# Where the on-chip buffers of a two-block transformer kernel begin: all large buffers moved to multiples of 2048 bytes, the arena to a multiple of 512

## The chip, the core and the metric

The kernel runs on one core of one Trainium2 chip. The metric is the device time of one execution in microseconds (us), as the median of several. A core has five engines that run side by side and wait for each other with semaphores: TensorE (PE in the profile; its weight loads are shown apart as PEld), VectorE (DVE), ScalarE (ACT), GpSimd (POOL) and SyncE (SP, which here only issues DMAs). On-chip memory (SBUF) has 128 partitions; a buffer takes the same byte range in each, so "begins at 16512" means byte 16512 of every partition. TensorE reads both operands of a matmul from SBUF, the stationary one with LDWEIGHTS and the moving one with MATMUL, and writes its sums to a bank of PSUM (2 KB in each partition).

## The reference, cut to what matters

Two transformer blocks at SEQ = 256 rows of D = 1024, all in float32:

```python
h = rms_norm(x, g_mix);  proj = h @ w_in                      # 1024 -> 8192
ya = rms_norm(diff_attention(qa, ka, va)) ;  yr = silu(gr) * rms_norm(retention(qr, kr, vr))
x = x + (sigmoid(gate_a) * (ya @ w_branch_diff) + sigmoid(gate_r) * (yr @ w_branch_ret)) @ w_out
x = x + square(relu(rms_norm(x) @ w_ff1)) @ w_ff2              # 1024 -> 4096 -> 1024
x = x + sigmoid(rms_norm(x) @ w_ple_gate) * (p @ w_ple)
x = rms_norm(x)                                                # end of block 1
x = x + 0.5 * (silu(n(x) @ w_gate) * (n(x) @ w_up)) @ w_down   # 1024 -> 2816 -> 1024
x = x + concat(mla(...), moba(...)) @ w_out2
x = x + 0.5 * (silu(n(x) @ w_gate2) * (n(x) @ w_up2)) @ w_down2
out = rms_norm(x)
```

## The kernel before, in words

**Precision.** A float32 matrix product is made from three matmuls of a rounded type (fp32r): each operand is split into a high and a low part, and high x high, high x low and low x high are summed in PSUM.

**Weights.** All weights go through one list of 164 units of up to 128 x 2048 float32 (1 MB each). SP loads unit u into `raw[u % 6]` (`load`, L324), two DMAs each; ScalarE copies it rounded into `w_hi[u % 4]` (`hi`, L909, instruction L917); VectorE writes the difference into `w_lo`, which lies on top of `raw` (`lo`, L1300, instruction L1306). The weights are the moving operands of the matmuls.

**Activations.** They are the stationary operands, 128 x 128 at a time. TensorE turns a 128 x 128 block by a transpose against the identity in `masks` (`turn`, L472, instruction L478) into a PSUM bank; ScalarE writes the rounded part (`split`, L923) and VectorE the rest (L1313). Each turned operand has a home of its own: `hA` and `hB` hold the 1024-wide operands of the projections, `fT` the inner activations of the three feed-forward layers on their way down, `pT` the operand of w_ple, `cT` those of the two up-projections of the latent attention (384 columns of weights at a time for the queries, 512 for keys and values).

**Products.** All weight products go through `products` (L455), whose matmul is L464. A "narrow" product has 512 (or 384, 288) weight columns and one PSUM bank per 128 rows; a "wide" one has 1024 columns of weights, and so two matmuls of 512 columns, into two banks, for each stationary operand. Every matmul has its own LDWEIGHTS. The order on each engine is written out by hand; TensorE waits for `lo_ready` of a unit, ScalarE and the SP queue wait for `unit_used`.

**Where buffers lie.** `sb` (L170) hands out addresses one after the other, each rounded up to 32 bytes, from `nc.sbuf_base` (16481) rounded up to 128, which is 16512. The order is `raw`, `w_hi`, `hA`, `hB`, `x`, `src`, `gain`, `junk`, then two small scratch buffers, `masks`, some twenty small vectors, and last the arena (L208), a region that the stages of the kernel use in turn through `lay` (L210). The start of the arena is whatever was left:

```python
    at = [-(-nc.sbuf_base // 128) * 128]                       # 16512
    raw = [sb(f"raw{s}", [P, UNIT]) for s in range(RAW_SLOTS)]
    arena = at[0]                                              # 160160
    fT0, fT1, act_r, act_f, pl_s, sg, pT0, pT1, p_sb, gain_mid = lay(arena, ("fT_hi", [P, 4, SEQ], f32r), ...)
    (cT0,), (cT1,) = (lay(named[where], ...) for where, name in (("qT", "cT_hi"), ("kT", "cT_lo")))
```

Summed up from these lines, with the remainders that matter:

| buffer | begins, before | modulo 2048 | modulo 64 | begins, after | modulo 2048 |
|---|---|---|---|---|---|
| raw0 (w_lo0) | 16512 | 128 | 0 | 18432 | 0 |
| w_hi0 | 65664 | 128 | 0 | 67584 | 0 |
| hA_hi / hB_hi | 98432 / 114816 | 128 | 0 | 100352 / 116736 | 0 |
| x, src, gain | 131200, 139392, 147584 | 128 | 0 | 133120, 141312, 149504 | 0 |
| masks | 154496 | 896 | 0 | 155648 | 0 |
| arena, fT_hi, qaT | 160160 | 416 | 32 | 160256 | 512 |
| act_f | 172448 | 416 | 32 | 172544 | 512 |
| pT_hi | 192928 | 416 | 32 | 193024 | 512 |
| cT_hi | 202400 | 1696 | 32 | 202496 | 1792 |

All blocks that a matmul takes from `hA`, `hB`, `fT`, `pT` and `cT` lie at multiples of 512 bytes from the start of their buffer, so each keeps the remainder modulo 64 of its buffer.

Of the kernel before, what the change touches and what calls it, by code (L numbers as in the profile page):

```python
# [28 lines left out]
P = 128  # L29
D, TB, SEQ = 1024, 2, 256  # L30
KT = D // P
EPS = 1e-6
BIG = 1e30
RAW_SLOTS, HI_SLOTS = 6, 4
UNIT = 2048
HALF = 512


DH, DHD = 8, 64
RH, RK, RV = 4, 128, 256  # L40
# [52 lines left out]
def work_batches():  # L93
# [16 lines left out]
    order += [("p",)]  # L110
    order += [("ff", i, tb) for i in range(DFF // HALF) for tb in range(TB)]
    order += [("ple", tb, h) for tb in range(TB) for h in range(2)]
# [46 lines left out]
def two_blocks(nc, x_d, p_d, g_mix, w_in, lam_q1, lam_k1, lam_q2, lam_k2, g_diff, g_ret, w_bd, w_br, w_out,  # L159
# [3 lines left out]
    f32, f32r, bf16, i32 = mybir.dt.float32, mybir.dt.float32r, mybir.dt.bfloat16, mybir.dt.int32  # L163
# [3 lines left out]
    at = [-(-nc.sbuf_base // 128) * 128]  # L167
    named = {}

    def sb(name, shape, dt=f32, where=None):  # L170

        size = (2 if dt == bf16 else 4) * int(np.prod(shape[1:]))
        if where is None:
            where = at[0]
            at[0] += -(-size // 32) * 32
        named[name] = where
        return nc.alloc_sbuf_tensor_at(name, shape, dt, offset=where)

    raw = [sb(f"raw{s}", [P, UNIT]) for s in range(RAW_SLOTS)]
    w_lo = [sb(f"w_lo{s}", [P, UNIT], f32r, named[f"raw{s}"]) for s in range(RAW_SLOTS)]  # L180
    w_hi = [sb(f"w_hi{s}", [P, UNIT], f32r) for s in range(HI_SLOTS)]

    hA = [sb(f"hA_{s}", [P, KT, SEQ], f32r) for s in ("hi", "lo")]
    hB = [sb(f"hB_{s}", [P, KT, SEQ], f32r) for s in ("hi", "lo")]
    x = sb("x", [P, TB, D])
    src = sb("src", [P, TB, D])
    gain = sb("gain", [P, D])
    junk = sb("junk", [P, D], bf16)
    vjunk = sb("vjunk", [P, P], bf16)
    rjunk = sb("rjunk", [P, RV], bf16)  # L190
    masks = sb("masks", [P, P + 2 * 384])
    ident, mask, negdist = masks[:, 0:P], masks[:, P:P + 384], masks[:, P + 384:P + 768]
    ss = sb("ss", [P, 2 * len(NORMS)])
    rs = sb("rs", [P, 2 * len(NORMS)])
    ms = sb("ms", [P, 2 * len(NORMS)])
# [6 lines left out]
    ssc, msc, rsc = (sb(n, [P, 4]) for n in ("ssc", "msc", "rsc"))  # L202
    mn = sb("mn", [P, 32, TB])
    sm = sb("sm", [P, 32, TB])
    rsm = sb("rsm", [P, 32, TB])
    qc = sb("qc", [P, DH, TB])
    gd = sb("gd", [P, P])
    arena = at[0]  # L208

    def lay(start, *parts):  # L210

        out = []
        for name, shape, *dt in parts:
            out.append(sb(name, shape, dt[0] if dt else f32, start))
            start += -(-4 * int(np.prod(shape[1:])) // 32) * 32
        assert start <= nc.sbuf_usable_end, (name, start)
        return out
# [6 lines left out]
    (gg,) = lay(arena, ("gg", [P, TB, D]))  # L224
    qk_tm = lay(named["yr"], ("qk_tm0", [P, TB, HALF]), ("qk_tm1", [P, TB, HALF]))
    lam_v, lam_w = lay(named["ga"], ("lam_v", [P, 4, DHD]), ("lam_w", [P, 2, DHD]))
# [6 lines left out]
    fT0, fT1, act_r, act_f, pl_s, sg, pT0, pT1, p_sb, gain_mid = lay(  # L233
        arena, ("fT_hi", [P, 4, SEQ], f32r), ("fT_lo", [P, 4, SEQ], f32r), ("act_r", [P, TB, HALF]),
        ("act_f", [P, TB, HALF]), ("pl_s", [P, TB, D]), ("sg", [P, TB, D]),
        ("pT_hi", [P, 2, SEQ], f32r), ("pT_lo", [P, 2, SEQ], f32r), ("p_sb", [P, TB, 256]), ("gain_mid", [P, D]))
# [19 lines left out]
    ctx = ExitStack()  # L256
    bank = [ctx.enter_context(nc.psum_tensor(f"bank{i}", [P, HALF], f32)) for i in range(8)]
    acc = lambda tb, c: bank[2 * tb + c]
# [64 lines left out]
    def _(sp):  # L323
# [22 lines left out]
        def load_x(tb, c):  # L346
            cols = slice(c * HALF, (c + 1) * HALF)
            sp.dma_start(x[:, tb, cols], x_d[tb * P:(tb + 1) * P, cols]).then_inc(x_in[2 * tb + c], 16)
# [1612 lines left out]
```

## Time and profile before

| what | value |
|---|---|
| median of 3 runs | 1025.52 us (1025.19 to 1025.67) |
| span of the profiled execution | 1023.8 us |
| time outside the span | 1.7 us |
| TensorE busy | 997.6 us, 97% |
| VectorE / ScalarE / GpSimd busy | 57% / 48% / 7% |
| DMA traffic | 179 MB, 175 GB/s on the mean |

The profile is one execution. "Busy" counts a matmul from its start to its modelled end, and matmuls overlap in the pipeline; how fast TensorE really goes is read from the distance between the starts of neighbouring matmuls in the timeline, not from the duration of one.

### The profile page before, as it was taken

Reading aid. Unit: us, or ns where it says so; the run is one execution under the profiler, and the core shown is the slowest. Engines: PE = TensorE matmul, PEld = TensorE weight load, DVE = VectorE, ACT = ScalarE, POOL = GpSimd, SP = SyncE. Lnnn points to the kernel's source line nnn. Section 1 sums busy time; section 2 is a strip of 40 time slices with the busy share of each in tenths; the row PEclk is TensorE's granted clock in tenths of the full one; section 3 lists DMA queues with packets and bytes.
Section 4 is the critical chain, followed back from the end, with each engine's and each line's share of the span. In section 5 each row is a group of like instructions: output and inputs, shape, how many; then the busy total and the mean of one; then the engine's idle time right before and its main releaser. Section 6 shows DMA issues by size and latency. Waiting matters only on the chain.

```text
span 1023.8 us, 12693 instructions
## 1 busy us (share of the span) xinstructions
PE 997.6 (97%) x4730; PEld 821.2 (80%) x4730; DVE 578.5 (57%) x700; ACT 489.3 (48%) x613; POOL 72.3 (7%) x95
## 2 busy tenths in 40 slices
PE   6999999999999999999999999999999999999997
PEld 4888788888888888888778888888877888888885
DVE  4655555487675455455775545447555675545443
ACT  5535455743364444435563434335557454343431
POOL 3000000040020000000320000001111000000000
PEclk9999999999999999999999999999999999999999
DMA  9755545435475454544655555545552165656531
GB/s 324 246 190 165 165 142 178 157 136 185 165 263 201 169 199 169 184 185 165 202 176 197 178 192 183 185 148 175 174 203 64 44 212 177 203 168 204 167 120 42
DMA packets 99744, 179.27 MB, mean 175 GB/s; under 512 B 5856, under 2 KB 53872, under 8 KB 99696
## 3 DMA queue, kind: packets, MB, share of 16 engines
q1 hardware_dynamic: 97424, 171.99, 49.8%
q0 software_dynamic: 1984, 6.30, 1.9%
q8 instruction: 31, 0.51, 0.2%
q10 hardware_dynamic: 288, 0.33, 0.2%
q14 instruction: 17, 0.14, 0.0%
HBM read 177.55 MB, written 1.05 MB: 174 GB/s over the span
## 4 chain that ended last, share of the span: by engine, by line
PE 93%; DVE 3%; ACT 1%; issue 1%; POOL 1%; DMA 1%; DVEq 0%; POOLq 0%; ACTq 0%
PE bank L464 84%; PE bank L478 5%; DVE w_lo L1306 1%; PE bank L514 1%; PE bank L513 1%; DMA masks<-const_masks 1%; PE bank L525 0%; ACT w_hi L917 0%; PE bank L526 0%; PE bank L527 0%; POOL rs L1810 0%; DVE hA_lo L1313 0%; POOL ms L1809 0%; DVE x L1558 0%; PE bank L791 0%
## 5 line engine op out<-in xcount | busy, mean ns | idle before, releaser
L1306 DVE TENSOR_TENSOR w_lo<-raw,w_hi 128x2048 fp32r<-128x2048 f32 (+2 forms) x163 | 371.1, 2281 | 225.9 <-ACT w_hi L917 225.9
L917 ACT ACTIVATE w_hi<-raw 128x2048 fp32r<-128x2048 f32 (+2 forms) x163 | 308.1, 1891 | 165.6 <-PE bank L464 160.2
L464 PE MATMUL bank<-w_hi,hA_hi 128*128 128x512 f32 (+1 forms) x880 | 342.7, 395 | 5.4 <-DVE w_lo L1396 3.0
L464 PE MATMUL bank<-w_hi,hA_lo 128*128 128x512 f32 (+1 forms) x880 | 337.2, 389 | 0.0
L464 PE MATMUL bank<-w_lo,hA_hi 128*128 128x512 f32 (+1 forms) x880 | 336.5, 388 | 0.0
L464 PEld LDWEIGHTS bank<-w_hi,hA_hi 128*128 128x128 f32 x880 | 165.4, 188 | 39.1 <-issue 4.7
L464 PEld LDWEIGHTS bank<-w_hi,hA_lo 128*128 128x128 f32 x880 | 165.5, 188 | 34.6
L464 PEld LDWEIGHTS bank<-w_lo,hA_hi 128*128 128x128 f32 x880 | 165.8, 188 | 32.4
L464 PE MATMUL bank<-w_hi,fT_hi 128*128 128x512 f32 x304 | 95.8, 396 | 0.0
L464 PE MATMUL bank<-w_hi,fT_lo 128*128 128x512 f32 x304 | 95.8, 396 | 0.0
L464 PE MATMUL bank<-w_lo,fT_hi 128*128 128x512 f32 x304 | 95.8, 396 | 0.0
L923 ACT ACTIVATE fT_hi<-bank 128x256 fp32r<-128x256 f32 (+1 forms) x60 | 23.4, 439 | 118.0 <-PE bank L478 118.0
L464 PEld LDWEIGHTS bank<-w_hi,fT_lo 128*128 128x128 f32 x304 | 57.1, 188 | 13.8
L464 PEld LDWEIGHTS bank<-w_lo,fT_hi 128*128 128x128 f32 x304 | 57.1, 188 | 13.7
L464 PEld LDWEIGHTS bank<-w_hi,fT_hi 128*128 128x128 f32 x304 | 56.9, 188 | 13.4
L1313 DVE TENSOR_TENSOR fT_lo<-bank,fT_hi 128x256 fp32r<-128x256 f32 (+1 forms) x60 | 27.1, 491 | 63.3 <-ACT fT_hi L923 63.1
L1809 POOL TENSOR_SCALAR ms<-ss 128x1 f32<-128x1 f32 x16 | 9.8, 612 | 633.6 <-ACT junk L941 633.5
L1146 ACT ACTIVATE act_r<-bank,rs 128x256 f32<-128x256 f32 x44 | 20.9, 476 | 57.3 <-PE bank L464 54.8
L1592 DVE SCALAR_TENSOR_TENSOR act_f<-bank,rs,act_r 128x256 f32<-128x256 f32 x44 | 21.2, 481 | 21.5 <-ACT act_r L1146 21.5
L941 ACT ACTIVATE junk<-x 128x1024 bf16<-128x1024 f32 x16 | 16.9, 1057 | 34.2 <-DVE x L1339 21.9
L970 ACT ACTIVATE L<-L,mn 128x128 f32<-128x128 f32 x64 | 28.4, 458 | 10.0 <-DVE mn L1353 10.0
L464 PE MATMUL bank<-w_hi,hB_hi 128*128 128x512 f32 x96 | 30.2, 396 | 0.0
(236 smaller groups left out, 757.6 us busy)
## 6 DMA issues: line engine op xcount, KB each, us to landing
raw<-in_w_in SPq DMA_DIRECT2D x76, 512.0 KB, 4.7
raw<-in_w_ff SPq DMA_DIRECT2D x64, 512.0 KB, 4.0
raw<-in_ffn_w_gate SPq DMA_DIRECT2D x44, 512.0 KB, 4.0
raw<-in_ffn_w_up SPq DMA_DIRECT2D x44, 512.0 KB, 4.9
raw<-in_ffn_w_down SPq DMA_DIRECT2D x44, 512.0 KB, 4.0
raw<-in_w_out SPq DMA_DIRECT2D x16, 512.0 KB, 4.3
raw<-in_w_branch_diff SPq DMA_DIRECT2D x8, 512.0 KB, 4.1
raw<-in_w_branch_ret SPq DMA_DIRECT2D x8, 512.0 KB, 3.7
```

Of the source, the lines that this page charges most:

```text
L464: mm = pe.matmul(o, a, w, start=first and t == 0 and m < len(outs), stop=last and t == n - 1 and m >= len(todo) - len(outs))
L478: mm = pe.transpose(work(name)[0:cols, col:col + rows], blk, ident)
L513: pe.matmul(b[:, 0:P], q[:, h, 0:P], k[:, h, 0:P], start=True, stop=True)
L514: pe.matmul(b[:, P:384], q[:, h, P:SEQ], k[:, h, :], start=True, stop=True).then_inc(score_done, 1)
L917: act.activation(w_hi[u % HI_SLOTS][:, 0:w], raw[u % RAW_SLOTS][:, 0:w], ACT.Copy).then_inc(hi_ready, 1)
L923: act.activation(dst, b, ACT.Copy).then_inc(split_hi, 1)
L941: act.activation(junk[:, :], x[:, tb, :], ACT.Square, accum_out=ss[:, n:n + 1]).then_inc(square_sum, 1)
L970: e = act.activation(L[:, m % 4, c], L[:, m % 4, c], ACT.Exp, bias=mn[:, m, tb:tb + 1], scale=-1.0, accum_out=sm[:, m, tb:tb + 1])
L1146: act.activation(act_r[:, tb, 0:SUB], up(tb)[:, 0:SUB], ACT.Silu, scale=inv_rms(norm, tb))\
L1306: vec.tensor_tensor(w_lo[u % RAW_SLOTS][:, 0:w], raw[u % RAW_SLOTS][:, 0:w], w_hi[u % HI_SLOTS][:, 0:w].bitcast(f32), ALU.subtract).then_i ...
L1313: vec.tensor_tensor(dst, b, hi.bitcast(f32), ALU.subtract).then_inc(work_out[WB[name] % 2], 1)
L1592: vec.scalar_tensor_tensor(out=act_f[:, tb, 0:SUB], in0=up(tb)[:, SUB:2 * SUB], scalar=rs[:, n:n + 1], in1=act_r[:, tb, 0:SUB], op0=ALU.mu ...
```

## The change

Only addresses change. The small vectors are allocated first, from 16512 to 18336; the next address is then rounded up to a multiple of 2048 (18432), and the large buffers follow in their old order. `masks` moves in front of `vjunk` and `rjunk`, and `rsm` stands last. The arena begins at the next multiple of 512. No instruction, wait, size or order is different.

```diff
+LINE = 2048
@@ two_blocks
-    raw = [sb(f"raw{s}", [P, UNIT]) for s in range(RAW_SLOTS)]
-    w_lo = [sb(f"w_lo{s}", [P, UNIT], f32r, named[f"raw{s}"]) for s in range(RAW_SLOTS)]
-    w_hi = [sb(f"w_hi{s}", [P, UNIT], f32r) for s in range(HI_SLOTS)]
-    (hA, hB, x, src, gain, junk, vjunk, rjunk, masks as below)
     ss = sb("ss", [P, 2 * len(NORMS)])
     rs = sb("rs", [P, 2 * len(NORMS)])
...
     mn = sb("mn", [P, 32, TB])
     sm = sb("sm", [P, 32, TB])
-    rsm = sb("rsm", [P, 32, TB])
     qc = sb("qc", [P, DH, TB])
     gd = sb("gd", [P, P])
-    arena = at[0]
+    at[0] = -(-at[0] // LINE) * LINE
+
+    raw = [sb(f"raw{s}", [P, UNIT]) for s in range(RAW_SLOTS)]
+    w_lo = [sb(f"w_lo{s}", [P, UNIT], f32r, named[f"raw{s}"]) for s in range(RAW_SLOTS)]
+    w_hi = [sb(f"w_hi{s}", [P, UNIT], f32r) for s in range(HI_SLOTS)]
+
+    hA = [sb(f"hA_{s}", [P, KT, SEQ], f32r) for s in ("hi", "lo")]
+    hB = [sb(f"hB_{s}", [P, KT, SEQ], f32r) for s in ("hi", "lo")]
+    x = sb("x", [P, TB, D])
+    src = sb("src", [P, TB, D])
+    gain = sb("gain", [P, D])
+    junk = sb("junk", [P, D], bf16)
+    masks = sb("masks", [P, P + 2 * 384])
+    vjunk = sb("vjunk", [P, P], bf16)
+    rjunk = sb("rjunk", [P, RV], bf16)
+    rsm = sb("rsm", [P, 32, TB])
+    arena = -(-at[0] // 512) * 512
```

## Rows read from the trace of the kernel before

**Rows 1.** The page: span, TensorE's share, and its granted clock in 40 slices.

```profile
span 1023.8 us, 12693 instructions
PE 997.6 (97%) x4730; PEld 821.2 (80%) x4730; DVE 578.5 (57%) x700; ACT 489.3 (48%) x613; POOL 72.3 (7%) x95
...
PEclk9999999999999999999999999999999999999999
```

**Rows 2.** The chain that ended last: whole span; then only 300 to 480 us.

```profile
PE 93%; DVE 3%; ACT 1%; issue 1%; POOL 1%; DMA 1%; DVEq 0%; POOLq 0%; ACTq 0%
...
by line: PE bank L464 96.1%; PE bank L478 4.1%
```

**Rows 3.** Busy time by stretch: PE, PEld, DVE, ACT, POOL, clock, DMA share, GB/s.

```profile
400.00:500.00 100.00, 100.00 (x461) 82.17 (x460) 54.65 (x45) 44.19 (x44) 6.61 (x6) 1.00 0.48 171
900.00:1000.00 100.00, 100.00 (x450) 82.02 (x449) 49.77 (x42) 41.38 (x42) 0.00 (x0) 1.00 0.50 164
```

**Rows 4.** Weight products by operand, shapes apart: count, busy us, mean ns, idle before.

```profile
L464 PE MATMUL bank<-w_hi,hA_hi 128*128 128x512 f32 x864 | 337.9, 397 | 5.4 <-DVE w_lo L1396 3.0 <-DVE hA_lo L1313 1.2 <-issue 1.0
...
L464 PE MATMUL bank<-w_lo,fT_hi 128*128 128x512 f32 x304 | 95.8, 396 | 0.0
...
L464 PE MATMUL bank<-w_lo,hB_hi 128*128 128x512 f32 x96 | 29.6, 390 | 0.0
...
L464 PE MATMUL bank<-w_lo,cT_hi 128*128 128x512 f32 x8 | 2.5, 396 | 0.0
L464 PE MATMUL bank<-w_lo,pT_hi 128*128 128x512 f32 x8 | 2.5, 395 | 0.0
```

**Rows 5.** TensorE's timeline in a wide product from fT: start us, us, what, count.

```profile
340.78 0.63 PE L464 MATMUL bank<-w_lo,fT_hi 128*128 128x512 f32 x2
...
341.72 0.63 PE L464 MATMUL bank<-w_hi,fT_hi 128*128 128x512 f32 x2
342.18 0.63 PE L464 MATMUL bank<-w_lo,fT_hi 128*128 128x512 f32 x2
```

**Rows 6.** The same in a wide product from hB.

```profile
230.25 0.61 PE L464 MATMUL bank<-w_hi,hB_hi 128*128 128x512 f32 x2
...
232.06 0.39 PE L464 MATMUL bank<-w_lo,hB_hi 128*128 128x512 f32 x1
```

**Rows 7.** The same in a narrow product from hA, a feed-forward layer's way up.

```profile
400.00 0.39 PE L464 MATMUL bank<-w_hi,hA_lo 128*128 128x512 f32 x1
...
401.59 0.39 PE L464 MATMUL bank<-w_hi,hA_hi 128*128 128x512 f32 x1
```

**Rows 8.** The same in the wide product from cT, up to the next line's start.

```profile
774.93 0.63 PE L464 MATMUL bank<-w_hi,cT_hi 128*128 128x512 f32 x2
...
776.33 0.33 PE L789 MATMUL bank<-mv,aT 128*128 128x64 f32 x2
```

**Rows 9.** The same in a product of 384 columns from cT.

```profile
757.79 0.34 PE L464 MATMUL bank<-w_hi,cT_lo 128*128 128x384 f32 x1
...
758.83 0.34 PE L464 MATMUL bank<-w_hi,cT_lo 128*128 128x384 f32 x1
```

**Rows 10.** The same in a product of 288 columns from hA, sixteen matmuls apart.

```profile
713.82 0.29 PE L464 MATMUL bank<-w_hi,hA_hi 128*128 128x288 f32 x1
...
715.95 0.29 PE L464 MATMUL bank<-w_lo,hA_hi 128*128 128x288 f32 x1
```

**Rows 11.** Transposes and splits by operand, shapes apart.

```profile
L478 PE MATMUL bank<-masks,act_f 128*128 128x128 f32 x152 | 21.8, 272 | 0.0
L478 PE MATMUL bank<-masks,src 128*128 128x128 f32 x144 | 20.6, 282 | 9.1 <-DMA masks<-const_masks 6.6 <-DVE src L1332 1.6 <-DVE src L1703 0.6
...
L1313 DVE TENSOR_TENSOR fT_lo<-bank,fT_hi 128x512 fp32r<-128x512 f32 x16 | 10.3, 687 | 17.4 <-ACT fT_hi L923 17.4
L923 ACT ACTIVATE fT_hi<-bank 128x512 fp32r<-128x512 f32 x16 | 8.7, 596 | 30.9 <-PE bank L478 30.9
L1313 DVE TENSOR_TENSOR hB_lo<-bank,hB_hi 128x512 fp32r<-128x512 f32 x12 | 7.8, 686 | 5.0 <-ACT hB_hi L923 4.9
...
L923 ACT ACTIVATE hB_hi<-bank 128x512 fp32r<-128x512 f32 x12 | 6.6, 592 | 12.8 <-PE bank L478 12.8
```

**Rows 12.** The chain from 0 to 20 us, its one DMA piece.

```profile
1.18 5.34 DMA masks<-const_masks
```

More of the change, by code:

```diff
@@ L177, in sb @@
         return nc.alloc_sbuf_tensor_at(name, shape, dt, offset=where)
-    raw = [sb(f"raw{s}", [P, UNIT]) for s in range(RAW_SLOTS)]
-    w_lo = [sb(f"w_lo{s}", [P, UNIT], f32r, named[f"raw{s}"]) for s in range(RAW_SLOTS)]
-    w_hi = [sb(f"w_hi{s}", [P, UNIT], f32r) for s in range(HI_SLOTS)]
[L183 to L192, printed above, removed]
     ss = sb("ss", [P, 2 * len(NORMS)])
@@ L204, in two_blocks @@
     sm = sb("sm", [P, 32, TB])
-    rsm = sb("rsm", [P, 32, TB])
     qc = sb("qc", [P, DH, TB])
     gd = sb("gd", [P, P])
-    arena = at[0]
+    at[0] = -(-at[0] // LINE) * LINE
[9 more added lines that the diff above has]
+    masks = sb("masks", [P, P + 2 * 384])
+    ident, mask, negdist = masks[:, 0:P], masks[:, P:P + 384], masks[:, P + 384:P + 768]
+    vjunk = sb("vjunk", [P, P], bf16)
+    rjunk = sb("rjunk", [P, RV], bf16)
+    rsm = sb("rsm", [P, 32, TB])
+    arena = -(-at[0] // 512) * 512
     def lay(start, *parts):
```

## Prediction

> **What bounds the kernel now.** I read the head of the page first: TensorE is busy for 997.6 of 1023.8 us, at a granted clock in the top tenth in every slice, which is the 2.4 GHz level [rows 1]. The chain that ended last says the same from the other side: 93% of it is TensorE, and between 300 and 480 us it is TensorE alone, nearly all of it the weight products of L464 [rows 2]. The table by stretch shows what stands behind TensorE: in two stretches of 100 us it is busy for all 100, while VectorE is busy for 50 to 55, ScalarE for 41 to 44 and the DMA engines for half [rows 3]. So whatever the new addresses do to VectorE, ScalarE or the transfers costs or brings nothing there, short of a slowdown to nearly twice, and whatever they do to the spacing of TensorE's matmuls counts in full.
>
> The question is then whether TensorE's spacing depends on where an operand begins. Busy time can't tell, since matmuls overlap; the starts in the timeline can. The matmuls to compare have 512 moving columns each.
>
> From `hB`, wide product: from 230.25 to 232.06 us there are 8 of them, 1.81 / 8 = 226 ns [rows 6]. From `hA`, narrow product: 400.00 to 401.59, 7 of them, 227 ns [rows 7]. From `fT`, wide product: 340.78 to 342.18, 6 of them, 1.40 / 6 = 233 ns [rows 5]. From `cT`, wide product: 774.93 to 776.33, 6 of them, 233 ns again [rows 8]. The mean durations of the groups show it for all of them: 396, 396 and 395 ns for w_lo with `fT`, `cT` and `pT`, and 390 for w_lo with `hB` [rows 4]. (The 397 of w_hi with `hA_hi` is no counterexample: first matmuls after a transpose, which take longer, fall into that group.)
>
> The product from `hB` and that from `fT` have the same form: two matmuls per stationary operand, the same banks, the same moving buffers, both at full clock. What differs is the stationary operand's home. `hA` and `hB` begin at a multiple of 64 bytes (remainder 0), and `fT`, `pT` and `cT`, all three in the arena, at 32 modulo 64. No 512-column matmul of L464 with an arena operand is in a group of the fast kind, and no group from outside the arena is of the slow kind.
>
> **The change part by part.** It removes and adds no instruction, DMA or wait, and moves none on any queue. It moves addresses, and I take each kind of reader in turn.
>
> *Arena operands of weight products.* The arena goes from 32 to 0 modulo 64, which is the remainder that `hA` and `hB` had, and with it `fT`, `pT`, `cT`. The matmuls with 512 columns are 3 x 304 from `fT`, 3 x 8 from `pT` and 3 x 8 from `cT` [rows 4], 960 in all. If the remainder is the cause, each is spaced like those of `hA`: 233.3 - 226.7 = 6.6 ns less (the two spacings as means of rows 5 and 8, and of rows 6 and 7). 960 x 6.6 ns = 6.3 us. All of these lie where TensorE sets the end; nothing is late behind them, since the weights of the next units come from engines that are half idle [rows 3]. I take -6.3 us.
>
> *Products of 384 columns from `cT`.* 36 matmuls; their spacing is 1.04 / 6 = 173 ns [rows 9]. The 288-column products from `hA`, which is outside the arena, take 2.13 / 16 = 133 ns [rows 10]. 173 - 133 = 40 ns for 96 columns is the clock's own 2.4 columns a nanosecond, so the 384-column products carry no extra from the arena: 0. This row speaks against my reading, since an operand at 32 modulo 64 costs nothing there; I have no reason for it, and it is why I don't go above 55% below.
>
> *Outside operands.* `hA`, `hB`, `raw`, `w_hi` go from 128 to 0 modulo 2048. No row shows a stationary operand at 0 modulo 2048. For the moving one the nearest is the 288-column product: its weight blocks lie 1152 bytes apart, so they begin at 128, 256, 384 and 0 modulo 512 in turn, and the spacing over sixteen of them is even at 133 ns. I take 0. The far end is the slower rival below.
>
> *Transposes.* They read their block from `act_f` (32 modulo 64) in 272 ns and from `src` (0 modulo 64) in 282 on the mean [rows 11], the latter with the waits of its first ones. An arena operand costs nothing there, and I take 0 for all transposes.
>
> *Attention matmuls.* Some 310 short ones read from the arena or beside it. I take 0; if each gained what the wide ones do it would be 2 us more, and as much less at the other end.
>
> *VectorE and ScalarE.* The split into `fT` takes 687 and 596 ns, that into `hB` 686 and 592 [rows 11]. At most 4 ns of 600 hang on the arena's remainder, beside idle time: 0.
>
> *Transfers.* On the chain they stand only at the start, with 5.34 us [rows 12]. Nothing in the trace gives a price for the address that a transfer writes; a tenth of that piece, half a microsecond to either side, is my bound, 0 what I take. The Trainium skill has a rule for it: "DMA: Bandwidth & Descriptors", under "How a descriptor splits into AXI transactions", says that transactions begin at multiples of 256 bytes and that a piece which doesn't start on one pays for an extra, partly used one. By that rule every weight row, written at 128 modulo 256 now, would be a little cheaper after the change; no row here shows it.
>
> Sum: 1023.8 - 6.3 = 1017.5 us of span. The profiled execution stands 1.7 us under the median of 1025.52, so the forecast is 1019.2 us.
>
> **The rivals.**
> *(A) The remainder is not the cause.* The spacing of 233 ns would then belong to something else that `fT`, `pT` and `cT` share and the change leaves as it is: they lie above 160 KB in the partition, farther from `raw` and `w_hi` than `hA` and `hB` do. For it: the 384-column products and the transposes, where the arena costs nothing. Against it: no row shows a cost that grows with distance. It gives 1025.5 us. The Trainium skill has a rule that comes out the same way: "SBUF — State Buffer", section "Door 1: The DMA port swizzle", says that SBUF is read in lines of 16 bytes and that only crossings of such lines cost. All starts here, before and after, are multiples of 32, so by that rule no address of this change could matter. The 7 ns between groups at 0 and at 32 modulo 64 speak against it.
>
> *(B) Slower: it is 128 modulo 512 that is good.* All 2880 fast matmuls of 512 columns (3 x 864 and 3 x 96, rows 4) have stationary and moving blocks at exactly that remainder, and none at 0. If a start at 0 modulo 512 brings the slow spacing, because both streams of TensorE then begin on the same place of the memory as the writes of the other engines do, `hA` and `hB` fall to 233 ns and `fT` stays there: 2880 x 6.6 = 19 us, 1044.5 us. It decides as soon as more than 960 of the matmuls from `hA` and `hB` lose 6.6 ns. Against it: the even spacing of the 288-column products.
>
> *(C) Both.* The arena gains, and some of the outside operands lose as much. It looks like (A) in the time and is counted with it.
>
> **How the numbers follow.** Forecast 55%, (A) with (C) 33%, (B) 12%. The forecast's own range is 1017 (short attention matmuls gain too, and half a microsecond at the start) to 1021.5 (two thirds of the matmuls gain). To leave out no more than 2 in 10 the range must take in (A), so it ends at 1026.5; (B) is left out. About 0.2% (2 us) is what a measurement of this kernel can tell from no change. Faster by more than that is the forecast, 0.55; within it is (A) and (C), 0.33; slower is (B), 0.12.
>
> **What would show it.** In the profile of the changed kernel: the timeline of a wide product from `fT` has starts 0.453 us apart for two matmuls instead of 0.467, and the mean of w_lo with `fT_hi` falls from 396 to about 389 ns; `hA` and `hB` groups stay at 390; the 384-column products stay at 173 ns apart. Under (A) the `fT` group still says 396. Under (B) the `hA` groups rise by 6 or 7 ns. I am wrong at the first step if the spacing from `fT` doesn't move, and wrong in the second if it moves and the time doesn't.

## The result, and the profile after

The changed kernel takes 1019.81 us on the median (1019.71 to 1020.10, four runs) beside 1025.60 us for the kernel before (1025.19 to 1025.76, four runs): a ratio of 0.9938, 95% interval 0.9926 to 0.9949, so 5.8 us faster. The forecast was 1019.2 us. The profiled execution has a span of 1018.0 us and stands 1.8 us under its own time.

The head of the page, to be read against rows 1:

```profile
span 1018.0 us, 12693 instructions
PE 992.1 (97%) x4730; PEld 821.4 (81%) x4730; DVE 578.5 (57%) x700; ACT 489.1 (48%) x613; POOL 72.3 (7%) x95
```

The same instructions, and the 5.8 us are gone from the span and, to 0.3 us, from TensorE's busy time. VectorE, ScalarE and GpSimd are busy as long as before to 0.2 us.

The weight products by operand (count, busy us, mean ns, idle before), against rows 4; the matmul's line is L467 now:

```profile
L467 PE MATMUL bank<-w_lo,hA_hi 128*128 128x512 f32 x864 | 332.0, 390 | 0.0
...
L467 PE MATMUL bank<-w_lo,fT_hi 128*128 128x512 f32 x304 | 93.6, 389 | 0.0
...
L467 PE MATMUL bank<-w_lo,hB_hi 128*128 128x512 f32 x96 | 29.7, 390 | 0.0
```

The same group from `hA` in the kernel before, which rows 4 leave out:

```profile
L464 PE MATMUL bank<-w_lo,hA_hi 128*128 128x512 f32 x864 | 331.7, 390 | 0.0
```

The group from `fT` has come down from 396 to 389 ns; `hA` and `hB` haven't moved. TensorE's timeline in a wide product from `fT` (start us, duration us, what, count), against rows 5:

```profile
340.44 0.62 PE L467 MATMUL bank<-w_lo,fT_hi 128*128 128x512 f32 x2
...
341.80 0.62 PE L467 MATMUL bank<-w_lo,fT_hi 128*128 128x512 f32 x2
```

Six matmuls lie between the two starts: 1.36 / 6 = 227 ns instead of 233. Summed over all starts of the two traces, the 912 matmuls from `fT` take 5.8 us less, those from `pT` and `cT` 0.2 us less, and those from `hA` and `hB` 0.5 us more; all other work takes 0.3 us less, and TensorE starts 0.1 us earlier. The 0.5 us are scatter: over the eight full-width kernels in which `hA` and `hB` have the narrow spacing (before, changed, and six of the runs below), these sums lie between 664.4 and 665.6 us. So the time went where the forecast said. Why it did is another matter: the forecast's reason was the remainder of the stationary operand modulo 64, and that reason fell in the first experiment.

### The profile page after: what moved, and what is told of

Its sections match the earlier page's. It is cut to its first block, busy times and chain, and to the rows that moved or that the text cites. A ratio compares the mean times of both kernels' runs of the same rounds, so it can differ in the third digit from the quotient of the medians.

```text
span 1018.0 us, 12693 instructions
## 1 busy us (share of the span) xinstructions
PE 992.1 (97%) x4730; PEld 821.4 (81%) x4730; DVE 578.5 (57%) x700; ACT 489.1 (48%) x613; POOL 72.3 (7%) x95
## 3 DMA queue, kind: packets, MB, share of 16 engines
q1 hardware_dynamic: 97424, 171.99, 48.7%
## 4 chain that ended last, share of the span: by engine, by line
PE 93%; DVE 3%; ACT 1%; issue 1%; POOL 1%; DMA 1%; DVEq 0%; POOLq 0%; ACTq 0%
PE bank L467 84%; PE bank L481 5%; PE bank L517 1%; PE bank L516 1%; DVE w_lo L1309 1%; DMA masks<-const_masks 1%; PE bank L528 0%; PE bank L530 0%; PE bank L529 0%; POOL rs L1813 0%; POOL ms L1812 0%; DVE x L1561 0%; PE bank L794 0%; PE bank L793 0%; DVE sg L1560 0%
## 5 line engine op out<-in xcount | busy, mean ns | idle before, releaser
L467 PE MATMUL bank<-w_hi,hA_hi 128*128 128x512 f32 (+1 forms) x880 | 343.0, 396 | 5.1 <-DVE w_lo L1399 3.0
L467 PE MATMUL bank<-w_hi,hA_lo 128*128 128x512 f32 (+1 forms) x880 | 337.1, 389 | 0.0
L467 PE MATMUL bank<-w_lo,hA_hi 128*128 128x512 f32 (+1 forms) x880 | 336.7, 389 | 0.0
L467 PEld LDWEIGHTS bank<-w_hi,hA_hi 128*128 128x128 f32 x880 | 165.4, 188 | 38.7 <-issue 4.7
L467 PEld LDWEIGHTS bank<-w_hi,hA_lo 128*128 128x128 f32 x880 | 165.6, 188 | 34.7
L467 PEld LDWEIGHTS bank<-w_lo,hA_hi 128*128 128x128 f32 x880 | 165.9, 188 | 32.4
L467 PE MATMUL bank<-w_hi,fT_hi 128*128 128x512 f32 x304 | 93.8, 390 | 0.0
L467 PE MATMUL bank<-w_lo,fT_hi 128*128 128x512 f32 x304 | 93.6, 389 | 0.0
L467 PE MATMUL bank<-w_hi,fT_lo 128*128 128x512 f32 x304 | 93.6, 389 | 0.0
L467 PEld LDWEIGHTS bank<-w_lo,fT_hi 128*128 128x128 f32 x304 | 57.1, 188 | 11.9
L467 PEld LDWEIGHTS bank<-w_hi,fT_lo 128*128 128x128 f32 x304 | 57.1, 188 | 11.9
L467 PEld LDWEIGHTS bank<-w_hi,fT_hi 128*128 128x128 f32 x304 | 56.8, 188 | 11.6
L1595 DVE SCALAR_TENSOR_TENSOR act_f<-bank,rs,act_r 128x256 f32<-128x256 f32 x44 | 21.2, 481 | 21.6 <-ACT act_r L1149 21.6
L944 ACT ACTIVATE junk<-x 128x1024 bf16<-128x1024 f32 x16 | 16.9, 1055 | 33.9 <-DVE x L1342 21.7
L467 PE MATMUL bank<-w_hi,hB_hi 128*128 128x512 f32 x96 | 30.2, 396 | 0.0
```

The source lines that it names most:

```text
L467: mm = pe.matmul(o, a, w, start=first and t == 0 and m < len(outs), stop=last and t == n - 1 and m >= len(todo) - len(outs))
L944: act.activation(junk[:, :], x[:, tb, :], ACT.Square, accum_out=ss[:, n:n + 1]).then_inc(square_sum, 1)
L1595: vec.scalar_tensor_tensor(out=act_f[:, tb, 0:SUB], in0=up(tb)[:, SUB:2 * SUB], scalar=rs[:, n:n + 1], in1=act_r[:, tb, 0:SUB], op0=ALU.mu ...
```

## The experiments

Eleven kernels ran. All but two compute the whole result. "The spacing" is the distance between the starts of neighbouring matmuls, of 512 columns unless it is said. The expected texts speak of theories: R is the forecast's reason, P the change's own multiples, D the difference between the two operands' starts, A a rule for each operand by itself. The moving operands are `raw` (with `w_lo` on top) and `w_hi`.

### The arena at a multiple of 64, nothing else

```diff
-    arena = at[0]
+    arena = -(-at[0] // 64) * 64
```

(on the kernel before)

> The kernel before with one edit: the arena begins at the next multiple of 64 bytes (160192 instead of 160160); all other buffers stay at 128 modulo 2048. Theory R (a 512-column weight matmul is spaced 6.6 ns wider when its stationary operand begins at 32 modulo 64, and nothing else in the change matters): the whole gain of the change, 5.8 us below the kernel before, about 1019.8 us; starts in a wide product from fT 227 ns apart. Theory P (the gain comes from the large buffers at multiples of 2048 or the arena at a multiple of 512): no change, 1025.6 us, and 233 ns apart.

Measured: 1026.40 us, ratio to the kernel before 1.0005 (0.9995 to 1.0014). The timeline in a wide product from `fT`:

```profile
340.90 0.63 PE L464 MATMUL bank<-w_lo,fT_hi 128*128 128x512 f32 x2
...
341.83 0.63 PE L464 MATMUL bank<-w_hi,fT_hi 128*128 128x512 f32 x2
...
342.77 0.40 PE L464 MATMUL bank<-w_hi,fT_lo 128*128 128x512 f32 x1
```

1.87 / 8 = 234 ns: as wide as before, with the arena at a multiple of 64. Theory R is wrong.

### The change without the arena's start

```diff
-    arena = -(-at[0] // 512) * 512
+    arena = -(-at[0] // 512) * 512 + 32
```

(on the changed kernel, as in all runs below unless it is said)

> The changed kernel with the arena 32 bytes further (160288, which is 32 modulo 64); the large buffers stay at multiples of 2048. Theory R: the change's gain is gone, 1025.6 us, fT matmuls 233 ns apart again, hA and hB at 227. Theory P for the large buffers: the gain stays, 1019.8 us. Theory of distance (what lies above 160 KB is slow) is already hard to hold after the change, and would see no difference here either: 1019.8 us.

Measured: 1025.87 us, ratio 1.0004 (0.9994 to 1.0014). The whole gain is gone with the large buffers still at multiples of 2048. The groups:

```profile
L467 PE MATMUL bank<-w_lo,hA_hi 128*128 128x512 f32 x864 | 331.9, 390 | 0.0
...
L467 PE MATMUL bank<-w_lo,fT_hi 128*128 128x512 f32 x304 | 95.8, 396 | 0.0
```

`fT` is back at 396 ns, `hA` is not touched. So the place of the arena is needed. The theory of distance is gone too, since 32 bytes of 160000 decide. Together with the first run: what counts is where the arena begins, but a multiple of 64 isn't enough.

### hA and hB 32 bytes off

```diff
+    at[0] += 32
     hA = [sb(f"hA_{s}", [P, KT, SEQ], f32r) for s in ("hi", "lo")]
     hB = [sb(f"hB_{s}", [P, KT, SEQ], f32r) for s in ("hi", "lo")]
+    at[0] = -(-at[0] // 64) * 64
     x = sb("x", [P, TB, D])
...
-    arena = -(-at[0] // 512) * 512
+    arena = -(-at[0] // 64) * 64
```

> The changed kernel with hA and hB alone 32 bytes further (32 modulo 64); moving operands and arena stay aligned to 64. Theory R: 2880 matmuls of 512 columns from hA and hB lose 6.6 ns each, 19 us: 1038.8 us; those of 288 and 384 columns from hA show whether the loss depends on the number of moving columns (none by the rows of cT with 384 columns); fT stays at 227 ns. If the loss belonged to something that only fT, pT and cT share (distance, their place in the arena): 1019.8 us.

Measured: 1041.19 us, ratio 1.0149 (1.0132 to 1.0165). The groups and the timeline:

```profile
L469 PE MATMUL bank<-w_lo,hA_hi 128*128 128x512 f32 x864 | 336.7, 396 | 0.0
...
L469 PE MATMUL bank<-w_lo,fT_hi 128*128 128x512 f32 x304 | 95.6, 396 | 0.0
...
L469 PE MATMUL bank<-w_lo,hA_hi 128*128 128x288 f32 x16 | 4.7, 292 | 0.0
```

The wide spacing isn't a property of the arena: `hA` has it now. But `fT` has it too, which this kernel was not meant to touch. Its arena begins at 160320, a multiple of 64 again and not of 128. Of the 21.4 us above the changed kernel, the starts give 14.9 to `hA` and `hB` and 6.2 to the arena's operands. The first is less than the 19 expected because not all of the 2880 were narrow: 2385 of them were at 228 ns or less in the changed kernel, and these take 6.5 ns more each, 15.6 us; the other 495 were wider already, 305 of them among the first six of a product behind transposes or attention work, and together they take 0.7 us less. The products of 288 columns lose nothing (292 ns; 295 in the kernel before).

### The moving operands 32 bytes off

```diff
-    at[0] = -(-at[0] // LINE) * LINE
+    at[0] = -(-at[0] // LINE) * LINE - 32
     raw = [sb(f"raw{s}", [P, UNIT]) for s in range(RAW_SLOTS)]
...
+    at[0] = -(-at[0] // 64) * 64
     hA = [sb(f"hA_{s}", [P, KT, SEQ], f32r) for s in ("hi", "lo")]
```

> The changed kernel with the moving operands alone, raw (w_lo) and w_hi, at 32 modulo 64 (from 18400); hA, hB, fT, pT, cT stay aligned. Theory R (the stationary operand's own remainder decides): 1019.8 us, all spacings as in the changed kernel. Theory D (it is the difference between the remainders of the stationary and the moving operand that costs): all 3840 matmuls of 512 columns lose 6.6 ns, 25 us: 1045 us. If the moving operand has a price of its own, something else, to be read from the spacings.

Measured: 1041.44 us, ratio 1.0152 (1.0135 to 1.0169).

```profile
L468 PE MATMUL bank<-w_lo,hA_hi 128*128 128x512 f32 x864 | 336.8, 396 | 0.0
...
L468 PE MATMUL bank<-w_lo,fT_hi 128*128 128x512 f32 x304 | 95.7, 395 | 0.0
```

Every stationary operand lies as in the changed kernel, and all are slow. The 21.6 us above the changed kernel are 15.1 from `hA` and `hB` and 6.1 from the arena's operands by the starts; the 25 expected counted all 3840 as narrow, and the 495 that were wider already (the run above) take no more here either. This ends every theory that looks at the stationary operand alone. Two are left: the two operands have to agree (D), or each has to be aligned to more than 64 (A).

### Everything 32 bytes off

```diff
-    at[0] = -(-at[0] // LINE) * LINE
+    at[0] = -(-at[0] // LINE) * LINE + 32
...
-    arena = -(-at[0] // 512) * 512
+    arena = at[0] // 512 * 512 + 32
```

> The changed kernel with every large buffer and the arena 32 bytes further: moving operands, hA and hB at 32 modulo 2048, arena at 544. The differences between any two of them stay what they are in the changed kernel (multiples of 512), but no start is a multiple of 64. Theory D (a matmul of 512 columns takes the wide spacing when its stationary and its moving operand differ in their remainder modulo 128 or more): 1019.8 us, all spacings 227 ns. Theory A (each operand has to begin at a multiple of 128 by itself): all 3840 matmuls are 6.6 ns wider, 25 us, 1045 us.

Measured: 1020.54 us, ratio 0.9943 (0.9926 to 0.9960).

```profile
L467 PE MATMUL bank<-w_lo,hA_hi 128*128 128x512 f32 x864 | 331.8, 390 | 0.0
L467 PE MATMUL bank<-w_lo,fT_hi 128*128 128x512 f32 x304 | 93.6, 389 | 0.0
```

No buffer of this kernel begins at a multiple of 64, and it has the whole gain. Theory A, which expected 1045 us, is out by 24 us. What decides is the difference between the start of the stationary and that of the moving operand.

### The arena at a multiple of 128, on the kernel before

```diff
-    arena = at[0]
+    arena = -(-at[0] // 128) * 128
```

> The kernel before with one edit: the arena begins at the next multiple of 128 (160256, 96 bytes further); the large buffers stay at 128 modulo 2048, so arena and moving operands differ by 384 modulo 512. If the modulus is 128 in either theory: the change's whole gain from 96 bytes, 1019.8 us. If the remainders have to agree modulo 256 or 512: no gain, 1025.6 to 1026 us.

Measured: 1026.09 us, ratio 1.0002 (0.9993 to 1.0012). The arena at 160256, the moving operands at 128 modulo 2048: a difference that is a multiple of 128, and no gain. The timeline from `fT`:

```profile
340.16 0.64 PE L464 MATMUL bank<-w_hi,fT_hi 128*128 128x512 f32 x2
...
342.95 0.39 PE L464 MATMUL bank<-w_hi,fT_hi 128*128 128x512 f32 x1
```

2.79 / 12 = 233 ns. The arena's start is the very one of the changed kernel, where it is fast: the same byte is a good or a bad place, depending on where the weights lie.

### A difference of 256

```diff
-    arena = -(-at[0] // 512) * 512
+    arena = -(-at[0] // 512) * 512 + 256
```

> The changed kernel with the arena 256 bytes further, so that the starts of arena and moving operands differ by 256 modulo 512. The arena 96 bytes further on the kernel before left a difference of 384 modulo 512 and brought nothing, so the modulus of theory D is 256 or 512. D with 256: 1019.8 us and fT matmuls 227 ns apart. D with 512: the gain is gone, 1025.6 us, about 233 ns apart.

Measured: 1019.97 us, ratio 0.9940 (0.9923 to 0.9957).

```profile
L467 PE MATMUL bank<-w_lo,fT_hi 128*128 128x512 f32 x304 | 93.6, 389 | 0.0
```

`fT` stays at 389 ns with a difference of 256, and it was slow with one of 128: among powers of two, the modulus is 256.

### The smallest edit that does it

```diff
-    arena = at[0]
+    arena = -(-(at[0] - 128) // 512) * 512 + 128
```

(on the kernel before)

> The kernel before with one edit: the arena begins at 128 modulo 512 (160384), which is the remainder that all its large buffers have; these stay where they were, at 128 modulo 2048. Theory D, with either modulus: the change's whole gain, 1019.8 us, though no large buffer begins at a multiple of 256, 512 or 2048. If the large buffers' own multiples of 2048 bring a part: the time stays above 1019.8 by that part.

Measured: 1019.75 us, ratio 0.9938 (0.9921 to 0.9954), the changed kernel's time.

```profile
L464 PE MATMUL bank<-w_lo,hA_hi 128*128 128x512 f32 x864 | 331.9, 390 | 0.0
L464 PE MATMUL bank<-w_lo,fT_hi 128*128 128x512 f32 x304 | 93.7, 389 | 0.0
```

The large buffers at multiples of 2048, which are most of the change's lines, are worth nothing by themselves. It is enough that the arena moves by 224 bytes, to the remainder that `raw` and `w_hi` have.

### raw alone 32 bytes off

```diff
-    at[0] = -(-at[0] // LINE) * LINE
+    at[0] = -(-at[0] // LINE) * LINE - 32
     raw = [sb(f"raw{s}", [P, UNIT]) for s in range(RAW_SLOTS)]
     w_lo = [sb(f"w_lo{s}", [P, UNIT], f32r, named[f"raw{s}"]) for s in range(RAW_SLOTS)]
+    at[0] += 32
     w_hi = [sb(f"w_hi{s}", [P, UNIT], f32r) for s in range(HI_SLOTS)]
```

> The changed kernel with raw alone, and w_lo on top of it, 32 bytes off (from 18400); w_hi, hA, hB and the arena stay. Of the three matmuls of a product only high x low then has a moving operand whose start differs from the stationary one's. Theory D priced per matmul: 1280 of the 3840 lose 6.6 ns, 8.4 us, 1028.2 us; and if the moving operand conflicts with the load of the next matmul's weights, it is the spacing behind the w_lo matmul that widens; if with its own weights' load, the spacing ahead of it.

Measured: 1034.39 us, ratio 1.0082 (1.0065 to 1.0099), 14.6 us above the changed kernel and not 8.4. The timeline from `fT`:

```profile
392.39 0.63 PE L468 MATMUL bank<-w_lo,fT_hi 128*128 128x512 f32 x2
392.86 0.62 PE L468 MATMUL bank<-w_hi,fT_lo 128*128 128x512 f32 x2
393.32 0.62 PE L468 MATMUL bank<-w_hi,fT_hi 128*128 128x512 f32 x2
393.77 0.63 PE L468 MATMUL bank<-w_lo,fT_hi 128*128 128x512 f32 x2
```

From the w_lo pair to the next start are 0.47 us, from the pair behind it 0.46, from the third 0.45, which is the undisturbed spacing. So it is the spacing behind the matmul that streams the odd operand that widens, and not the one ahead of it. The weight loads show what else happens in that stretch:

```profile
392.17 0.41 PEld L468 LDWEIGHTS bank<-w_lo,fT_hi 128*128 128x128 f32 x2
392.63 0.42 PEld L468 LDWEIGHTS bank<-w_hi,fT_lo 128*128 128x128 f32 x2
```

The weights for the matmul that starts at 392.86 load from 392.63 on, while the second w_lo matmul streams. (The records of the loads themselves don't get longer: 188 ns on the mean in this kernel as in the changed one.)

Against the changed kernel, the spacings behind the 1280 w_lo matmuls are 8.4 us longer in sum, which is just what I expected. Those behind the matmuls that follow them, w_hi with the low part of the activation, are 4.4 us longer, and those behind the third kind 1.8 us, though neither of these streams an odd operand. My sum left out that the disturbance outlasts its matmul, and so one odd operand in three costs two thirds of what three cost. Why it lasts is not shown.

### Fewer columns

In two kernels the feed-forward layers' way down leaves out columns: 448 of 512 in the first layer, 384 in the second, 256 in the third. One has the arena 32 bytes off, the other as changed.

```diff
-    products([acc(tb, c)[:, :] for c in range(2)], fT, ...)        # first layer
+    products([acc(tb, c)[:, 0:448] for c in range(2)], fT, ...)
-    products([acc(tb, c)[:, :] for c in range(2)], fT, ...)        # second and third
+    products([acc(tb, c)[:, 0:384 if name == "f1" else 256] for c in range(2)], fT, ...)
```

> The changed kernel with the arena at 32 modulo 64 (as in the second run), and with narrower matmuls where fT is the stationary operand: the first feed-forward layer's way down uses 448 of each 512 columns, the second's 384, the third's 256; the other columns are left out. It asks why products of 384 columns showed no cost. If the cost belongs to 512 columns alone or grows with the columns, spacing against the next kernel's: a few ns more at 448, 0 at 384 and 256. If the cost is one of the narrow product from cT only, 6 ns at every width.

> The same narrower matmuls (448, 384 and 256 columns; the rest left out) with the arena at a multiple of 512, as in the changed kernel. Spacing N / 2.4 + 13.3 ns in every width, as 226.7 for 512, 173.3 for 384 and 133.3 for 288: 200 ns at 448, 173 at 384, 120 at 256, unless the weight load sets it at 256.

Measured: 973.11 us with the arena off, 972.92 with it as changed; one time each. First the groups of the kernel with the arena off, then those of the other:

```profile
L467 PE MATMUL bank<-w_lo,fT_hi 128*128 128x448 f32 x128 | 36.5, 366 | 0.0
L467 PE MATMUL bank<-w_lo,fT_hi 128*128 128x384 f32 x88 | 22.4, 336 | 0.0
L467 PE MATMUL bank<-w_lo,fT_hi 128*128 128x256 f32 x88 | 17.6, 281 | 0.0
```

```profile
L467 PE MATMUL bank<-w_lo,fT_hi 128*128 128x448 f32 x128 | 36.3, 365 | 0.0
L467 PE MATMUL bank<-w_lo,fT_hi 128*128 128x384 f32 x88 | 22.5, 336 | 0.0
L467 PE MATMUL bank<-w_lo,fT_hi 128*128 128x256 f32 x88 | 17.7, 283 | 0.0
```

The cost is one of full 512-column matmuls: 1 ns at 448, nothing at 384, and at 256 those from the odd arena are even shorter by 2 ns. The medians of the spacings, arena off and as changed: 203 and 203 ns at 448, 173 and 173 at 384, 118 and 120 at 256. Lengths between 448 and 512 were not tried. This is what rows 9 had shown and what I had no reason for: they were no evidence against the operands' addresses, they were matmuls of a length that doesn't feel them. At 448 columns the spacing is 3 ns above the 200 I expected from the other lengths, whatever the arena does; why is open.

## Why the prediction was right

**What bounds the kernel.** Right: TensorE's spacing went into the time in full. In the runs that are slower the same holds up to 21 us.

**Which matmuls.** Right: 960 of 512 columns from `fT`, `pT` and `cT`, 233 to 227 ns. The size was 6.3 us against 5.8 measured. By the starts these 960 gave 6.0, which leaves 0.3 of the missing 0.5 to them: 22 of the 911 spacings from `fT` are still above 228 ns. The other 0.2 us are within the scatter of the rest of the kernel.

**The cause.** Wrong, although the number came out: that was luck. The step that failed is "What differs is the stationary operand's home", taken by its remainder modulo 64; what counts is the difference between the starts of the stationary and the moving operand, modulo 256. In the kernel before both readings fit every group of 512 columns, since all moving operands lay at 128 modulo 256 and there were only two kinds of stationary ones. All runs at full width together (starts modulo 256, spacing in ns; the kernel with `raw` alone off has two rows at the end):

| kernel | moving | stationary | difference | spacing |
|---|---|---|---|---|
| before, hA and hB | 128 | 128 | 0 | 227 |
| before, fT | 128 | 160 | 32 | 233 |
| changed, all | 0 | 0 | 0 | 227 |
| arena at a multiple of 64 | 128 | 192 | 64 | 234 |
| arena 32 off | 0 | 32 | 32 | 233 |
| hA and hB off | 0 | hA 32, fT 64 | 32, 64 | 234 |
| weights off | 224 | 0 | 32 | 234 |
| all 32 off | 32 | 32 | 0 | 227 |
| arena at a multiple of 128 | 128 | 0 | 128 | 233 |
| arena 256 off | 0 | 0 | 0 | 227 |
| arena only | 128 | 128 | 0 | 227 |
| raw off, behind w_lo | 224 | 0 | 32 | 234 |
| raw off, behind the two w_hi | 0 | 0 | 0 | 230, 229 |

The wide rows of `fT` differ by less than they seem to: the means over all its starts are 233.0 ns for a difference of 128, 233.6 for 64, 233.4 to 233.6 for 32.

Had the change moved the arena alone, to a multiple of 64 or 128, I would have forecast the same gain and been wrong; two runs show it. That the forecast held is owed to the edit, which took both operands to multiples of 512.

**Rival (A), the remainder is not the cause.** In its title it came true: the stationary operand's remainder alone is not the cause. In its time it did not, since the change did move what is. Its evidence, the 384-column products, has the explanation above. The rule named beside it, in "SBUF — State Buffer" of the Trainium skill, section "Door 1: The DMA port swizzle", is that accesses within a 16-byte line get full bandwidth and a crossing to a new line costs. It does not account for what is measured here: all starts of all runs are multiples of 32, and the time moves by 21.7 us, from 1019.75 to 1041.44.

**Rival (B), slower.** Excluded: starts at 0 modulo 512 are fast with moving operands at 0, and those at 0 are slow with moving ones at 128. Its mechanism looked at the places of both streams of TensorE, though against the writes of other engines, and so was nearer to what the runs show than my forecast's, with the sign turned round: it is good when the two begin at the same place. Its price of 19 us for `hA` and `hB` is above what they cost in the runs with them or the weights off, 15 us.

**What I took as zero.** The transposes read in 272 and 282 ns as in rows 11; the splits of VectorE in 686 ns, those of ScalarE in 594 to 596. The DMA piece on the chain at the start went from 5.34 us [rows 12] to 5.26:

```profile
1.18 5.26 DMA masks<-const_masks
```

The weight queue's share of the DMA engines over the span fell from 49.8% before to 48.7% in the changed kernel, which writes the weights to 0 modulo 256 and no longer to 128. Its line in the changed kernel, and in the one with the arena 32 bytes off, whose weights go to the same addresses:

```profile
q1 hardware_dynamic: 97424, 171.99, 48.7%
```

```profile
q1 hardware_dynamic: 97424, 171.99, 49.8%
```

So the share moves by as much with the weights in the same place, and it can't be put down to their address. The rule of "DMA: Bandwidth & Descriptors" in the Trainium skill, section "How a descriptor splits into AXI transactions", by which a piece that starts off a multiple of 256 bytes costs more, is thus neither shown nor refuted by these two lines. It does not reach the time of this kernel: the one with the arena alone moved still writes weights to 128 modulo 256 and takes 1019.75 us, beside 1019.81.

**Still open.** Why a difference in the starts costs TensorE some 16 cycles of 2.4 GHz a matmul (6.6 ns) is not shown; only that it arises in the stretch in which one operand streams and the next weights load, at 512 columns. That the two reads get in each other's way is the reading that suggests itself, not one that a run singles out. Differences of 32, 64 and 128 were measured; others between 0 and 256, and steps under 32 bytes, were not tried; nor was an agreement at a remainder other than 0, 32 and 128.

## What to carry to other kernels

When two groups of matmuls have the same form and different spacing, look at where their operands begin, both of them, before looking at waits: here the starts in the timeline gave 6 us that no busy share, wait or chain shows. Lay the homes of stationary and moving operands so that they agree modulo 256 bytes, for every buffer that feeds a full 512-column matmul (a multiple of 256 for all of them does it); a rule for one buffer alone, as "a multiple of 64" or "of 128", may bring nothing. And a forecast that fits nearly all rows may still have the wrong cause: move one buffer at a time, and then all of them together, to learn whether a place or a difference counts.

## What the runs showed of the hardware that was not expected

- Spacing of fp32r matmuls with 512 columns, a new stationary operand each time: 227 ns when the starts of both operands agree modulo 256 bytes, 233 to 234 ns when they differ by 32, 64 or 128.
- It is relative: with everything at 32 modulo 64 the kernel takes 1020.54 us, with only the weights there 1041.44.
- The cost is in full-length matmuls only: 1 ns at most at 448 columns, none at 384, 288 and 256.
- A disturbed matmul disturbs the next ones too: one odd operand in three costs 14.6 us, of which 8.4 behind its own matmuls; all three cost 21.6.
